# RWKV-7 recurrence of a two-layer decoder block: the triangular inverse moved from 64x64 to 32x32 tiles

## What is computed

```python
def step(S, inp):
    r_t, w_t, k_t, v_t, a_t, b_t = inp
    sa = jnp.einsum('bhvk,bhk->bhv', S, a_t)
    S = S * w_t[:, :, None, :] + sa[..., None] * b_t[:, :, None, :] + v_t[..., None] * k_t[:, :, None, :]
    return S, jnp.einsum('bhvk,bhk->bhv', S, r_t)
_, out = lax.scan(step, S0, xs)
```

```python
p = jax.nn.softmax(jnp.concatenate([s_meta, s_band, sink], axis=-1), axis=-1)
o = (jnp.einsum('bnkgqm,bmkd->bnqkgd', p_meta, v_meta)
     + jnp.einsum('bnkgqj,bnjkd->bnqkgd', p_band, v_band))
```

## Time and profile before

| | |
|---|---|
| median of 3 runs | 1660.3 us (1658.23 to 1662.76) |
| the profiled execution's own time | 1661.37 us |
| its span, first to last instruction | 1659.6 us |
| mean granted TensorE clock | 0.992 |
| TensorE matmul busy | 1624.7 us, 98% of the span |
| weight load busy | 1387.9 us, 84% |
| VectorE, ScalarE, GpSimd busy | 1250.4 us, 977.4 us, 103.2 us |
| instructions in the trace | 27774 |

### The profile page before, as it was taken

How to read it: one execution, slowest core, us unless ns; L and a number is a source line. 1 busy time by engine, 2 the same in 40 slices (tenths; PEclk the granted TensorE clock), 3 DMA queues, 4 the chain that set the end, 5 groups by cost and what they waited for, 6 DMA issues and landing times.

```text
span 1659.6 us, 27774 instructions
## 1 busy us (share of the span) xinstructions
PE 1624.7 (98%) x11505; PEld 1387.9 (84%) x11505; DVE 1250.4 (75%) x1178; ACT 977.4 (59%) x987; POOL 103.2 (6%) x151
## 2 busy tenths in 40 slices
PE   9999999999998999999999999999999999999997
PEld 7879999999677985788888888888888888888886
DVE  5655655545676734788988988988898988998987
ACT  5665434431433222667767767677676767767765
POOL 3463000001003100000000000000000000000000
PEclk9999999999999999999999999999999999999999
DMA  8115555542430006499999999999999999999994
GB/s 283 52 52 180 177 177 178 178 158 78 152 137 17 4 4 241 159 374 378 360 358 349 372 355 382 365 349 356 367 366 375 363 350 357 368 364 377 362 367 187
DMA packets 191617, 432.68 MB, mean 261 GB/s; under 512 B 10051, under 2 KB 11075, under 8 KB 191492
## 3 DMA queue, kind: packets, MB, share of 16 engines
q1 hardware_dynamic: 191452, 430.82, 72.6%
q10 hardware_dynamic: 40, 0.08, 0.0%
HBM read 429.82 MB, written 1.05 MB: 260 GB/s over the span
## 4 chain that ended last, share of the span: by engine, by line
PE 93%; DVE 4%; ACT 2%; issue 1%; ACTq 0%; POOL 0%; DVEq 0%; POOLq 0%
PE ps L1377 18%; PE ps L1379 18%; PE ps L1378 18%; PE ps L711 6%; PE ps L713 6%; PE ps L712 6%; PE ps L960 4%; PE ps L1270 2%; PE ps L1401 1%; PE ps L1093 1%; PE ps L1108 1%; PE ps L970 1%; PE ps L1330 1%; DVE arena L2210 1%; DVE wsplit L2393 0%
## 5 line engine op out<-in xcount | busy, mean ns | idle before, releaser
L2393 DVE TENSOR_TENSOR wsplit<-raw_w,wsplit 128x2048 fp32r<-128x2048 f32 x336 | 751.3, 2286 | 78.5 <-ACT wsplit L1813 78.5
L1813 ACT ACTIVATE wsplit<-raw_w 128x2048 fp32r<-128x2048 f32 x336 | 624.9, 1919 | 59.4 <-PE ps L1379 59.4
L1377 PE MATMUL ps<-wsplit,xsplit 128*128 128x512 f32 x896 | 354.2, 395 | 0.0
L1379 PE MATMUL ps<-wsplit,xsplit 128*128 128x512 f32 x896 | 349.5, 390 | 0.0
L1378 PE MATMUL ps<-wsplit,xsplit 128*128 128x512 f32 x896 | 348.9, 389 | 0.0
L1379 PEld LDWEIGHTS ps<-wsplit,xsplit 128*128 128x128 f32 x896 | 168.1, 188 | 35.8
L1378 PEld LDWEIGHTS ps<-wsplit,xsplit 128*128 128x128 f32 x896 | 168.5, 188 | 33.2
L1377 PEld LDWEIGHTS ps<-wsplit,xsplit 128*128 128x128 f32 x896 | 168.3, 188 | 33.4 <-DVE wsplit L2393 0.5
L1377 PE MATMUL ps<-wsplit,hsplit 128*128 128x512 f32 x448 | 175.2, 391 | 1.5 <-DVE hsplit L2423 1.5
L1378 PE MATMUL ps<-wsplit,hsplit 128*128 128x512 f32 x448 | 174.4, 389 | 0.0
L1379 PE MATMUL ps<-wsplit,hsplit 128*128 128x512 f32 x448 | 174.4, 389 | 0.0
(11 more groups left out here) (415 smaller groups left out, 2247.3 us busy)
## 6 DMA issues: line engine op xcount, KB each, us to landing
raw_w<-in_moe_w_gate SPq DMA_DIRECT2D x114, 1024.0 KB, 7.1
raw_w<-in_moe_w_up SPq DMA_DIRECT2D x112, 1024.0 KB, 7.8
raw_w<-in_moe_w_down SPq DMA_DIRECT2D x112, 1024.0 KB, 7.2
ffn_raw<-in_ffn_w_up SPq DMA_DIRECT2D x14, 1024.0 KB, 5.2
ffn_raw<-in_ffn_w_gate SPq DMA_DIRECT2D x14, 1024.0 KB, 5.1
ffn_raw<-in_ffn_w_down SPq DMA_DIRECT2D x14, 1024.0 KB, 5.1
ffn_raw<-in_attn_w_qkv SPq DMA_DIRECT2D x6, 1024.0 KB, 11.1
ffn_raw<-in_attn_w_o SPq DMA_DIRECT2D x4, 1024.0 KB, 11.1
```

The lines of the kernel that those rows point to most:

```text
L1377: mm(o, x_[0], w_[0], start=first_, stop=False)
L1379: return mm(o, x_[1], w_[0], start=False, stop=last_)
L1813: A(wsplit[:, m % NRING, 0, :], raw_w[:, m % NRAW, :], ACT.Copy).then_inc(w_hi, 1)
L2393: v.tensor_tensor(wsplit[:, m % NRING, 1, :], raw_w[:, m % NRAW, :], wsplit[:, m % NRING, 0, :].bitcast(F32), ALU.subtract).then_inc(w_lo, 1)
```

## The change

On the recurrence:

- A new kind of chunk product, AA (`diagonal`), computes only the 32x32 diagonal blocks of BA for each head, two products per head and chunk, into a compact array `A32` of 32 columns per pair; VectorE masks it, adds the unit matrix, makes the first approximation and transposes it, all on 32 instead of 64 columns per pair. BA stays for chunks 1 to 4, without the unit matrix, and falls away for chunk 0.
- The levels up to block size 32 (3 for chunk 0, 4 for the others: `N32`) work on 32x32 tiles: each Y and each X of a chunk is 32 products, on the four diagonal 32x32 tiles of the array, with half as many columns to evict and to transpose.
- The last level of chunks 1 to 4 is done blockwise: the two diagonal blocks are turned by products with the identity into the full 64 columns (`whole_diagonal`, 32 products), Y is one 32x32 product per head (16), and X one more per head (16). Chunk 0 has only the `whole_diagonal`.
- The masks get a compact 32-column form (`mask32`) inside `mask64`.

On the attention: 5 identity products into bank 6 ahead of the value products of the first six head pairs.

The diff, cut to its core:

```diff
-        NLV = [3] + [5] * (NCH - 1)
+        N32 = [3] + [4] * (NCH - 1)
+        NLV = [n + 1 for n in N32]
+        ROWS32 = [slice(g * 32, (g + 1) * 32) for g in range(4)]
...
+                if c < 6:
+                    filler(5, 6)
                 values(c)
...
+            def diagonal(c):
+                b = group("AA", c)
+                for p, e, rows, toks in heads:
+                    for k in range(2):
+                        t = slice(c * CH + 32 * k, c * CH + 32 * (k + 1))
+                        o = ps[ROWS32[2 * tok(p, e) + k], b + p % 2, (p // 2) * 32:(p // 2 + 1) * 32]
+                        last = mm(o, b_a[rows, p, t], kk_a[rows, p, t], start=True, stop=True)
+                last.then_inc(grp_mm, 1)
...
             for c in range(NCH):
-                products("BA", c)
+                diagonal(c)
+                if c:
+                    products("BA", c)
                 products("KA", c)
...
+                if l < N32[c]:
+                    for p in range(PAIRS):
+                        for rows in ROWS32:
+                            last = mm(ps[rows, n % 4, p * 32:(p + 1) * 32], A32[rows, c * PAIRS + p, :], X[rows, c * PAIRS + p, :],
+                                      start=True, stop=True)
+                else:
+                    whole_diagonal(l, c)
+                    for p in range(PAIRS):
+                        for h in range(2):
+                            upper, lower = ROWS32[2 * h], ROWS32[2 * h + 1]
+                            last = mm(ps[lower, n % 4, p * 32:(p + 1) * 32], BAa[c][upper, p, 32:CH], X[upper, c * PAIRS + p, :],
+                                      start=True, stop=True)
...
+            def whole_diagonal(l, c):
...
                 for p in range(PAIRS):
-                    for rows in HROWS:
-                        last = mm(ps[rows, n % 4, p * CH:(p + 1) * CH], BAa[c][rows, p, :], X[rows, c * PAIRS + p, :],
-                                  start=True, stop=True)
-                last.then_inc(y_mm, 1)
+                    for h in range(2):
+                        upper, lower = ROWS32[2 * h], ROWS32[2 * h + 1]
+                        wide_ = CH if c == 0 else 32
+                        mm(ps[upper, 4 + n % 4, p * CH:p * CH + wide_], X[upper, c * PAIRS + p, :],
+                           ident[upper, h * CH:h * CH + wide_], start=True, stop=True)
+                        last = mm(ps[lower, 4 + n % 4, p * CH:(p + 1) * CH], X[lower, c * PAIRS + p, :],
+                                  ident[lower, h * CH:(h + 1) * CH], start=True, stop=True)
+                return last
...
                 for p in range(PAIRS):
-                    for rows in HROWS:
-                        o = ps[rows, 4 + n % 4, p * CH:(p + 1) * CH]
-                        x_, y_ = XT[rows, c * PAIRS + p, :], Y[rows, c, p, :]
-                        last = mm(o, y_, x_, start=True, stop=True) if l == NLV[c] - 1 else mm(o, x_, y_, start=True, stop=True)
+                    if l < N32[c]:
+                        for rows in ROWS32:
+                            last = mm(ps[rows, 4 + n % 4, p * 32:(p + 1) * 32], XTc[rows, c * PAIRS + p, :], Y[rows, c, p, :],
+                                      start=True, stop=True)
+                    else:
+                        for h in range(2):
+                            upper, lower = ROWS32[2 * h], ROWS32[2 * h + 1]
+                            last = mm(ps[upper, 4 + n % 4, p * CH + 32:(p + 1) * CH], Y[lower, c, p, :],
+                                      XTc[lower, c * PAIRS + p, :], start=True, stop=True)
                 last.then_inc(x_mm, 1)
```

More of the change, by code:

```diff
@@ L385, in build @@
         for c in range(NCH):
-            for kind in ("BA", "KA", "TB", "TK", "TV"):
-                if c == NCH - 1 and kind in ("TB", "TK"):
+            for kind in ("AA", "BA", "KA", "TB", "TK", "TV"):
+                if c == NCH - 1 and kind in ("TB", "TK") or c == 0 and kind == "BA":
                     continue
                 G[kind, c] = len(EVICTED)
-                n_dve, n_act = n_dve + (2 if c else 1) * (kind[1] == "A"), n_act + (kind[0] == "T")
+                n_dve, n_act = n_dve + (2 if c and kind != "AA" else 1) * (kind[1] == "A"), n_act + (kind[0] == "T")
                 EVICTED.append((kind[0] == "T", n_act if kind[0] == "T" else n_dve))
@@ L588, in compact, with compact32 @@
                     one(g.tensor_copy(mask64[rows, n, :], wide[rows, rows]))
+            def compact32(n, src):
+                for rows in ROWS32:
+                    one(g.tensor_copy(mask32[rows, n, :], src[rows, rows]))
+            fill(mask64[:, 2:8, :], 0.0)
             def unit():
@@ L598, in _ @@
                 compact(j)
-            for l in range(2, 7):
+            compact32(M_STRICT, wide)
+            for l in range(2, 6):
                 b = 1 << (l - 1)
@@ L1090, in level_y @@
                     pe.wait_ge(x0_ok, c + 1)
[L1091 to L1095 removed]
+                if l < N32[c]:
[10 more added lines that the diff above has]
+                                      start=True, stop=True)
+                last.then_inc(y_mm, 1)
+            def whole_diagonal(l, c):
+                n = NX[l, c]
+                if n >= 4:
+                    pe.wait_ge(x_act, n - 3)
+                pe.wait_ge(x_act, NX[l - 1, c] + 1)
+                for p in range(PAIRS):
+                    for h in range(2):
[6 more added lines that the diff above has]
+                return last
             def level_x(l, c):
                 n = NX[l, c]
[L1099 removed]
+                if l == N32[c] and c == 0:
+                    whole_diagonal(l, c).then_inc(x_mm, 1)
+                    return
+                if l < N32[c] and n >= 4:
                     pe.wait_ge(x_act, n - 3)
@@ L2203, in _, with over32 @@
             causal = mask64[:, 0:2, :].unsqueeze(1).to_broadcast([P, 4, 2, CH])
+            def over32(n):
+                return mask32[:, n, :].unsqueeze(1).to_broadcast([P, PAIRS, 32])
             for c in range(NCH):
+                cc = slice(c * PAIRS, (c + 1) * PAIRS)
+                g = G["AA", c]
+                dve.wait_ge(grp_mm, g + 1)
+                strict = mask32[:, M_STRICT, :].unsqueeze(1).unsqueeze(1).to_broadcast([P, 2, 4, 32])
+                own.done(v.tensor_tensor(by_parity(A32[:, cc, :]),
+                                         ps[:, 2 * (g % 4):2 * (g % 4) + 2, 0:P].rearrange("p y (q i) -> p y q i", q=4), strict,
+                                         ALU.mult), grp_dve)
+                own.settle()
+                own.done(v.tensor_tensor(A32[:, cc, :], A32[:, cc, :], over32(M_UNIT), ALU.add), dve_own)
+                own.settle()
+                own.done(v.tensor_tensor(XTc[:, cc, :], A32[:, cc, :], over32(M_FIRST), ALU.mult), dve_own)
+                own.settle()
+                v.transpose(X[:, cc, :].rearrange("p a b -> p (a b)"), XTc[:, cc, :].rearrange("p a b -> p (a b)")).then_inc(x0_ok, 1)
                 for n, kind in enumerate(("BA", "KA")):
+                    if c == 0 and n == 0:
+                        continue
                     g = G[kind, c]
```

53 lines of the change are left out of this document (28 added, 25 removed).

## The result

The changed kernel takes 1707.51 us (median of 4 runs, 1705.92 to 1709.16) against 1661.53 us for the kernel before (4 runs, 1658.23 to 1662.82). The ratio is 1.0279, with a 95% interval of 1.0263 to 1.0295. The change makes the kernel 46 us slower. The prediction said 1707.

A forecast was written before the change was run, and what follows sets the result against it. TensorE's instruction fetch, 128 weight load and matmul pairs per 3.73 us, was taken as the bound. Recurrence +48, attention -2, clock after the levels +1 give +47 us: 1708.4 profiled, 1707 us median, range 1692 to 1719.

The forecast's parts named there:

- The fetch as the bound: Recurrence: TensorE can't issue more than 128 weight load and matmul pairs in 3.73 us, however small; chance 0.83.
- rival (b): Recurrence: instruction fetch is hidden, the stops local or a trace artefact; levels 28 us, kernel 1640 us; chance 0.08.
- The count: Recurrence: 1024 matmuls in the chunk products and 3008 in the levels, 4032 together, two for each small product.
- rival (e): Recurrence: a 32x32 product is one matmul, so instructions don't double; 2368 matmuls, about 1658 us, no change; chance 0.02.
- The price of a block: Recurrence: 3.73 us for each 128 matmuls, 30.4 blocks, 113.5 us; bounds 3.6 to 3.9 us a block.
- The 0.6 us added for waits: Recurrence: some 40 semaphore waits take places in the instruction blocks, +0.6 us.
- +48: Chunk products and levels together: +47.5 us from the instruction fetch and +0.6 us for semaphore waits, taken as +48.
- +1: Solves after the levels: they may begin at the lower clock, +1 us, bounds 0 and +4.
- The attention: Identity products cost +1.4 us uncovered but may keep the clock up; net -2 us, bounds -6 and +3.
- VectorE, ScalarE, GpSimd: Recurrence: evictions and transposes shrink to roughly half, masks need more small copies; all covered, no effect on the time.
- Rival (d): Recurrence: VectorE's and ScalarE's latency adds to the fetch stops, 0.6 us for each of 31 blocks, +18, 1725; chance 0.05.

The follow-up runs named there:

- the repeat: The changed kernel, unaltered, run again on the chip of the next three runs: 1704.80 us, ratio 1.0271 to the kernel before.
- the first execution: The changed kernel as first profiled, nothing altered: 1708.78 us, against 1661.37 for the profiled kernel before.

## Why the prediction was right

**The fetch as the bound** held. The prediction named it from a stop of 1.24 us and four packets; after the change the stops are the largest entry of the chain, 128 matmuls apart, the queue has the 107 packets foretold, and the run with independent small products shows the limit by itself. The fetch being hidden, rival (b), would have made the levels 28 us and six blocks of small products about 6 us; they are some 86 and 20.6. One reading in the prediction went too far: that the levels of before run just at this limit. They came evenly at 3.73 us for 128 matmuls, without stops, which the later runs show to be above the fetch's 3.45; the sum does not use it. The Trainium skill's rule that dispatch is slower than the fill ("Runtime: NRT & Kernel Launch", section "Instruction fetch mechanics") does not hold for these tiles: TensorE stood for 1.5 to 2.6 us with nothing to issue. The other rule, "TensorEngine Tiling (Array Packing)", section "Instruction Overhead", warned against small tiles rightly, but not for the reason that it gives: 136 matmuls in 1.34 us at 2.4 GHz are 10 ns each, where 60 cycles would be 25. They take turns on four tiles, so an overhead that overlaps between tiles is not excluded by this.

**The count** held to the instruction: 1024 and 3008 matmuls, so a 32x32 product is two matmuls and rival (e) is out.

**The price of a block** was 3.73 us in the sum. The repeat and the first execution took 113.5 and 113.9 us from the first product to the end of the levels; the same code took 116.9 us without the identity products. With 136 matmuls free and 30.4 blocks, the forecast for it was 116.9. The term was 3 us too high for the two executions of the change: from the second block's start to the end of the levels both needed 3.60 us a block. In the timeline of the repeat the distances from stop to stop fall mostly near 3.46 and near 3.75 us, in about equal numbers, with a few up to 4.0. The forecast's 3.73 was the second of these values and not the mean, and that its distances agreed to 0.01 us was partly chance. Why there are such steps stays open. The 116.9 without the identity products is no sign of a dearer block, since the levels took 86.0 us there and the surplus is in the chunk products. The 0.6 us added for waits was not needed.

**Stage by stage**, cut as in the earlier trace rows: chunk products 27.9 us (some 28 foretold), levels 85.9 (about 87). Together they became 44.4 us longer, against +48 foretold. From the end of the levels to the experts' first product it was 87.2 us before and 88.7 after, +1.5 against +1, with the clock at its lower level until 645.1.

**The attention** was the term with the wrong sign in the profiled execution: -2 foretold, and its end came 1.0 us later than before (128.20 against 127.21), after a front that was 1.1 us early, so +2.1. The condition that the prediction set, the clock at its full level from 74 to 108 us or else a loss, is what the two executions of one kernel showed: the attention took 58.3 us in the repeat, with the clock full, and 62.9 in the first, against 60.8 in the kernel before. Over runs the identity products gain 1.8 us in the kernel before and 6.5 in the changed one, 3.4 of which lie in the recurrence and not in the attention. The value of -2 is about right as a mean, but for the last two places alone: the other four cost what they give. Why the gain in the changed kernel was larger, and whether the phase in which the recurrence meets its first packet has to do with it, was not tried.

**VectorE, ScalarE, GpSimd**: nothing of their savings or additions reached the path, as assumed. Rival (d), latencies adding to the stops, did not happen: in the groups of the levels VectorE ended 0.9 us of the idle time ahead of L1123, "issue" 12.0.

So 44.4 + 1.5 + 2.1 - 1.1 = 46.9, which is the 47.0 us between the spans. The forecast of +47 has the same total by 48 - 2 + 1. Two errors of 3 to 4 us, in the block price and in the attention, cancelled in the profiled execution, so a match to 1 us is luck. The profile of the repeat, where the attention came out as foretold, is 43.1 us longer than that of the kernel before, 4 under the forecast of 47; its median is 45.3 us longer than that of the kernel before on the same chip. The mechanism and the count were right, and the price of a block was the term that was too large.

## What to carry to other kernels

Before cutting products into smaller tiles, count TensorE's instructions and not its columns: in this kernel 128 pairs of weight load and matmul took about 3.45 us at best where they came densely, so a long row of tiles that the array finishes in less than about 27 ns a pair gains nothing, and twice as many of them cost nearly twice the time. The same small products between long ones made no stop. Stops of TensorE called "issue" at equal distances, beside single packets in the instruction queue, are the mark of this, and a few of them in a stage that looks bound by something else are enough to forecast from. In such a stage, removing instructions (a flag in place of opening products) pays where faster engines around it do not.

## What the runs showed of the hardware

- At the lower clock, fp32 products on 64x64 tiles took 52 to 53 ns a matmul whether 32 or 64 columns moved; at the full clock 29 ns with 64.
- The granted clock stayed at 1.2 GHz through 154 us in which TensorE's matmul side was busy without a gap (64x64 tiles, 32 moving columns), while in the kernel before, on the same tiles with 64 moving columns, it was low from 548.5 to 551.9 us and then back at 2.4 GHz. A busy PE is thus no promise of the full clock.
- 32x32 matmuls on four tiles in turn took 15 ns each at the lower clock (128 in 1.93 us) and some 10 ns at the full clock (136 in 1.34 us); from start to start it is 13.3 and 8.5 ns.
- The distance of two blocks was 3.45 us, once 3.73, where TensorE had only independent small products, and 3.60 us in the mean in the change, with single ones up to 4.0 and above; what adds to it stays open. Nor was it tried to move work with few instructions, such as projections, between the levels' products, which these numbers suggest: TensorE stands idle there for about 36 of 86.7 us.
